# Hybrid decoder step: Delta heads and retention or mLSTM heads in turn

## What is computed

```
x += rms(W_out [mLSTM | retention | gated Delta](rms(x)))
x += rms(W_down relu(W_up rms(x))^2)

# a Delta head, per chunk
q3,k3,v3 = split(silu(conv4(q,k,v)));  q = l2norm(q3)*d**-.5;  k = l2norm(k3)
A   = strict(decay) * beta * k k^T
sol = (I + A)^-1 [beta*gamma*k, beta*v];  U = Ut - W S
o   = gamma * q S + (q k^T * decay) U
S   = exp(G) S + (k * decay)^T U
```

## Time and profile before

| | us |
|---|---|
| median of 3 runs (lowest, highest) | 3278.93 (3278.43, 3280.37) |
| the profiled execution | 3280.49 |
| its span, first to last instruction | 3278.9 |
| mean granted TensorE clock | 0.987 of full speed |
| head quads, one layer | about 40 to 675 |
| weight loads (256 KB each) | 1669, 3.7 from issue to landing |

### The profile page before, as it was taken

One profiled execution on the slowest core, in us unless ns is written; L12 is line 12 of the kernel. 1 busy time (PEld: TensorE's weight loads), 2 busy tenths in 40 slices (PEclk: granted clock), 3 DMA queues, 4 the chain that ended last, 5 costly groups with the idle time before them and its releaser, 6 DMA issues.

```text
span 3278.9 us, 72394 instructions
## 1 busy us (share of the span) xinstructions
PE 3122.5 (95%) x23264; PEld 3057.9 (93%) x23264; DVE 1930.1 (59%) x3923; ACT 1535.4 (47%) x3564; POOL 84.5 (3%) x161
## 2 busy tenths in 40 slices
PE   5999999998999999999869999999989999999997
PEld 5989999998999999999869989999989999999997
DVE  5677755656545545455567777556665455454555
ACT  4566654544433334334446666545444333343333
POOL 0000000000000000000010000000000000000000
PEclk9999999999999999999989999999999999999999
DMA  3344455643544444544423444555435444444454
GB/s 132 128 133 135 132 162 161 185 155 110 175 166 159 164 164 166 166 160 164 151 84 121 131 132 137 168 167 177 155 118 167 165 164 167 162 163 164 163 167 147
DMA packets 266061, 499.24 MB, mean 152 GB/s; under 512 B 34272, under 2 KB 39552, under 8 KB 265664
## 3 DMA queue, kind: packets, MB, share of 16 engines
q1 hardware_dynamic: 243360, 443.56, 41.3%
q0 software_dynamic: 14496, 51.05, 4.7%
q10 hardware_dynamic: 8064, 2.80, 0.3%
HBM read 475.30 MB, written 22.01 MB: 152 GB/s over the span
## 4 chain that ended last, share of the span: by engine, by line
PE 79%; DVE 9%; ACT 5%; issue 4%; DMA 2%; DVEq 1%; ACTq 0%; SPq 0%; POOLq 0%; POOL 0%
PE PU L455 71%; PE PABCD L455 4%; PE PE_ L455 2%; ACT Y L787 2%; PE PF L455 2%; ACT AE L787 1%; DVE WL L1156 1%; DMA RAW<-in_w 1%; ACT WH L787 1%; DVE Y L1170 1%; PE PABCD L458 1%; DVE Y L1321 1%; DVE AE L1500 1%; DVE X L1173 0%; PE PE_ L458 0%
## 5 line engine op out<-in xcount | busy, mean ns | idle before, releaser
L455 PE MATMUL PU<-HH,WH 128*128 128x288 f32 x4096 | 1285.4, 314 | 59.3 <-DVE HL L1161 48.0
L787 ACT ACTIVATE WH<-RAW 128x512 fp32r<-128x512 f32 x1669 | 965.2, 621 | 591.9 <-PE PU L455 437.5
L455 PE MATMUL PU<-HL,WH 128*128 128x288 f32 x4096 | 1212.6, 296 | 0.0
L455 PE MATMUL PU<-HH,WL 128*128 128x288 f32 x4096 | 1208.7, 295 | 0.0
L1156 DVE TENSOR_TENSOR WL<-RAW,WH 128x512 fp32r<-128x512 f32 x1668 | 1074.5, 687 | 223.0 <-ACT WH L787 205.8
L455 PEld LDWEIGHTS PU<-HH,WH 128*128 128x128 f32 x4096 | 774.6, 189 | 79.2 <-DVE HL L1161 49.4
L455 PEld LDWEIGHTS PU<-HL,WH 128*128 128x128 f32 x4096 | 775.8, 189 | 7.0
L455 PEld LDWEIGHTS PU<-HH,WL 128*128 128x128 f32 x4096 | 775.0, 189 | 0.0
L455 PE MATMUL PU<-UH,WH 128*128 128x288 f32 x2560 | 759.0, 296 | 3.2 <-DVE UL L1310 2.0
L455 PE MATMUL PU<-UL,WH 128*128 128x288 f32 x2560 | 755.2, 295 | 0.0
L455 PE MATMUL PU<-UH,WL 128*128 128x288 f32 x2560 | 752.7, 294 | 0.0
(11 more groups left out here) (245 smaller groups left out, 2244.4 us busy)
## 6 DMA issues: line engine op xcount, KB each, us to landing
RAW<-in_w SPq DMA_DIRECT2D x1669, 256.0 KB, 3.7
SIN<-in_sin POOLq DMA_DIRECT2D x32, 512.0 KB, 4.2
out_sout<-Y POOLq DMA_DIRECT2D x32, 512.0 KB, 5.3
BC<-gate_rows POOLq DMA_DIRECT2D x32, 304.0 KB, 4.3
AUX<-in_aux POOLq DMA_DIRECT2D x32, 152.0 KB, 3.4
X<-in_x SPq DMA_DIRECT2D x4, 576.0 KB, 7.5
out_y<-X SPq DMA_DIRECT2D x4, 576.0 KB, 2.8
Y<-in_gw POOLq DMA_DIRECT2D x2, 1024.0 KB, 5.0
```

What stands on the lines that cost most here:

```text
L455: return nc.tensor.matmul(out, lhsT, rhs, start=start, stop=stop, skip_group_check=True)
L787: return nc.scalar.activation(out, in_, f, **kw)
```

## The change

`walk` now pairs the heads: a Delta head's quad, then a retention head's (first four pairs) or an mLSTM head's (next three), with the front of the next Delta head in it. The last pair is Delta head 7's quad, without a front, and mLSTM head 3 in the first "out" quad. `par` is 0 for every Delta head and 1 for every other. Weights, states and parameters stay in memory where they were, so SP and POOL take their addresses from the new order; TensorE waits for the output blocks by `turn_of`. The silu semaphore is split in two.

```diff
-                def gdn_pair(i, last):
-                    for par in range(2):
-                        h = 2 * i + par
-                        after = None if last and par else (n0 + h + 1, l * H_C + h + 1, h + 1, 1 - par, p0 + i + par)
-                        quad(q0 + 1 + h, "gdn", l, (n0 + h, l * H_C + h, h, par, p0 + i), after)
...
-                with eng.Fori(0, H_B // 2) as i:
-                    for par in range(2):
-                        h = 2 * i + par
-                        quad(q0 + 1 + H_C + h, "ret", l, (n0 + H_C + h, l * H_B + h, h, par, p0 + H_C // 2 + i))
-                for h in range(H_A - 1):
-                    quad(q0 + 1 + H_C + H_B + h, "mls", l, (n0 + H_C + H_B + h, l * H_A + h, h, h % 2, p0 + (H_C + H_B + h) // 2))
...
+                def pair(i, other, k):
+
+                    g0 = l * H_C
+                    quad(q0 + 1 + 2 * i, "gdn", l, (n0 + 2 * i, g0 + i, i, 0, p0 + i))
+                    quad(q0 + 2 + 2 * i, other, l, (n0 + 2 * i + 1, l * H_B + k, k, 1, p0 + i),
+                         (n0 + 2 * i + 2, g0 + i + 1, i + 1, 0, p0 + i + 1))
+
+                with eng.Fori(0, H_B) as i:
+                    pair(i, "ret", i)
+                for i in range(H_B, H_C - 1):
+                    pair(i, "mls", i - H_B)
+                i = H_C - 1
+                quad(q0 + 1 + 2 * i, "gdn", l, (n0 + 2 * i, l * H_C + i, i, 0, p0 + i))
+                last_head = (n0 + 2 * i + 1, l * H_A + H_A - 1, H_A - 1, 1, p0 + i)
...
+        def turn_of(k):
+
+            return 2 * k if k < H_C else 2 * (k - H_C) + 1
...
+            with sp.Fori(0, DEPTH) as l:
+                q0, u0 = l * QUADS, l * (4 * QUADS)
+
+                with sp.Fori(0, H_C - 1) as i:
+                    next_units(q0 + 2 * i, u0 + 4 * i, u0 + 4 * (H_C + i))
+                    next_units(q0 + 2 * i + 1, u0 + 4 * (H_C + i), u0 + 4 * (i + 1))
...
-                if next_head:
+                if next_at is not None:
 
                     held("head_done", n + 1)
-                    load_parameters(n + 1, 1 - par)
-                    load_rows(n + 1, 1 - par)
...
+                    load_parameters(next_at, 1 - par)
+                    load_rows(next_at, 1 - par)
...
-                            pe.wait_ge(sem("ul_ready"), ul_before(l, kind, x[0]) + k + 1)
+                            pe.wait_ge(sem("ul_ready"), ul_before(l, kind, x[0]) + (turn_of(k) if kind == "out" else k) + 1)
...
-                    tt(HHD[:], YY, Z[par][:, 3], ALU.mult).then_inc(sem("y_gated"), 1)
+                    tt(HHD[:], YY, Z[par][:, 3], ALU.mult).then_inc(sem(f"{silu}_y_gated"), 1)
```

More of the change, by code:

```diff
@@ L344, in _, with next_units @@
                 sp.dma_start(con[n][:], d[n]).then_inc(sem("constants_in"), 16)
-            with sp.Fori(0, DEPTH * QUADS) as Q:
+            def next_units(Q, unit, after):
                 for s in range(4):
@@ L349, in _ @@
                         sp.wait_ge(sem("lo_ready"), 16 * Q + 4 * s + c + 1)
-                        load(c, 4 * Q + s + 1)
+                        load(c, unit + s + 1 if s < 3 else after)
+            with sp.Fori(0, DEPTH) as l:
[3 more added lines that the diff above has]
+                    next_units(q0 + 2 * i + 1, u0 + 4 * (H_C + i), u0 + 4 * (i + 1))
+                i = H_C - 1
+                next_units(q0 + 2 * i, u0 + 4 * i, u0 + 4 * (H_C + i))
+                next_units(q0 + 2 * i + 1, u0 + 4 * (H_C + i), u0 + 4 * HEADS)
+                with sp.Fori(HEADS, QUADS) as q:
+                    next_units(q0 + q, u0 + 4 * q, u0 + 4 * (q + 1))
             sp.wait_ge(sem("lo_ready"), 16 * DEPTH * QUADS + 1)
@@ L382, in load_state, with head @@
                 pool.dma_start(SIN[:].rearrange("p b e -> p (b e)"), one("sin", n)).then_inc(sem("state_in"), 16)
-            def head(l, n, pair, par, next_head):
-                if next_head:
+            def head(n, at, next_at, pair, par):
+                if next_at is not None:
                     held("head_done", n + 1)
-                    load_parameters(n + 1, 1 - par)
-                    load_rows(n + 1, 1 - par)
-                if next_head:
+                    load_parameters(next_at, 1 - par)
+                    load_rows(next_at, 1 - par)
+                if next_at is not None:
                     held("state_decayed", n + 1)
                     held("state_read", n + 1)
-                    load_state(n + 1)
+                    load_state(next_at)
                 held("state_ready", n + 2)
-                pool.dma_start(one("sout", n)[:, HD:], CDEC.rearrange("p b e -> p (b e)")).then_inc(sem("state_out"), 16)
+                pool.dma_start(one("sout", at)[:, HD:], CDEC.rearrange("p b e -> p (b e)")).then_inc(sem("state_out"), 16)
                 held("state_out", 16 * (n + 1))
@@ L441, in _ @@
                 pool.dma_start(NG0[:], one("ng0", l + 1)).then_inc(sem("first_gain_in"), 16)
-                with pool.Fori(0, (H_C + H_B) // 2) as i:
-                    for par in range(2):
-                        head(l, n0 + 2 * i + par, p0 + i, par, True)
-                for h in range(H_A):
-                    head(l, a0 + h, p0 + (H_C + H_B) // 2 + h // 2, h % 2, h < H_A - 1)
+                with pool.Fori(0, H_C - 1) as i:
+                    head(n0 + 2 * i, n0 + i, n0 + H_C + i, p0 + i, 0)
+                    head(n0 + 2 * i + 1, n0 + H_C + i, n0 + i + 1, p0 + i, 1)
+                i = H_C - 1
+                head(n0 + 2 * i, n0 + i, n0 + H_C + i, p0 + i, 0)
+                head(n0 + 2 * i + 1, n0 + H_C + i, None, p0 + i, 1)
             pool.wait_ge(sem("first_gain_in"), 16 * (DEPTH + 1))
@@ L920, in head_scale, with linear_head @@
                 fn(GATE[:], LG[:], ACT.Exp, scale=-1.0).then_inc(sem("head_scale"), 1)
-            def linear_head(step, kind, x, last):
+            def linear_head(step, kind, l, x, last):
                 n, nk, hk, par, pair = x
@@ L1077, in gdn_head @@
                 if t == 27:
-                    store_prompt_state(n)
+                    store_prompt_state(n, l * HEADS + hk)
                     act.wait_ge(sem("gdn_out"), nk + 1)
@@ L1086, in mixer @@
                 if kind == "gdn":
-                    gdn_head(t, x)
+                    gdn_head(t, l, x)
                 elif kind in ("ret", "mls"):
@@ L1093, in mixer @@
                         if t == slot:
-                            linear_head(step, kind, x, last)
+                            linear_head(step, kind, l, x, last)
                 elif kind == "first":
@@ L1405, in linear_head @@
                     finish_log(n)
-                    y = finish_rest(n, par, not mls)
+                    y = finish_rest(n, par, None if mls else kind)
                     if not mls:
-                        dve.wait_ge(sem("y_gated"), silu_count(l, kind, hk))
+                        dve.wait_ge(sem("ret_y_gated"), nk + 1)
                     store_u(n, l, chunk_of(kind, hk), y)
@@ L1478, in gdn_tail @@
                 n, nk, hk, par, pair = x
-                y = finish_rest(n, par, True)
-                dve.wait_ge(sem("y_gated"), silu_count(l, "gdn", hk))
+                y = finish_rest(n, par, "gdn")
+                dve.wait_ge(sem("gdn_y_gated"), nk + 1)
                 store_u(n, l, chunk_of("gdn", hk), y)
```

15 lines of the change are left out of this document (4 added, 11 removed).

## The result

The changed kernel took **3285.70 us** (median of 14 runs, 3283.35 to 3288.21), the kernel before 3279.37 (14 runs): a ratio of **1.0017, 95% interval 1.0010 to 1.0025**, so 6.3 us slower. The forecast was 3269.5 and faster. The range, 3252 to 3294, holds the result; the direction was wrong. A second comparison, on another chip, gave 1.0014 (1.0005 to 1.0023).

The account below looks back on a forecast made before the run. TensorE was taken as the bound, busy for 95% of the span, with removable waits. -47.0 + 14.4 + 19.2 + 3.9 = -9.5 us from 3280.49 gave 3271.0, less 1.56 for the median: 3269.5 us; range 3252 to 3294.

Parts of the forecast that it names:

- The pool: TensorE's waits at four lines, 39.2 us listed in 49 waits, 47.0 us with 0.16 added each, all taken off.
- Retention quads: Eight retention quads with a front: new TensorE waits of 0.1 and 1.7 us, 1.8 us each, 14.4 us in all.
- excluded `WL`: Unit matmuls would not wait for WL; if they did, the weights' own chain had slipped and the forecast was wrong.
- The Delta quad near 41 us: Sign of being right: a Delta quad, 44.60 us long before the change, would take near 41 us.
- near 36: Sign of being right: a retention quad, 33.97 us long before the change, would take near 36 us.
- the root is then no longer late: Delta quad behind a fronted retention quad: root ready at 482.4, wanted at 480.9 + 1.7, so no further wait.
- mLSTM quads: Six mLSTM quads with a front: waits of 0.45, 1.5 and 1.2 us, 3.2 us each, 19.2 us in all.
- Out quad: First slot of two out quads: TensorE waits 1.9 us for Delta head 7's tail, 3.9 us in all.
- A: Rival: VectorE sets the fronted quads, 4 us each, +13 us, 3292 us; decides from 3.1 us per quad; chance 0.23.
- B: Rival: no change; full durations instead of spacings make CUR and UL about 0.7 us later, +10, 3279 us; chance 0.27.
- C: Rival: much faster; fronts find gaps in short quads, new waits half the size, -26, 3253 us; chance 0.16.
- The rule weighed: Skill: improve the busiest engine (no gain here), or interleave regimes (gain); trace bears out the latter for 1.4% of span.

Follow-up runs that it names:

- control run: The changed kernel unaltered, run once more beside the second group of experiments: 3288.11 us, 1.0014 of the kernel before.
- e4_cur_early: Changed kernel with CUR written in slot 22 instead of 31 of the 14 fronted retention and mLSTM quads: 3287.63 us, ratio 1.0003 to the kernel before.
- e2_v_one_tap: Changed kernel with three of the four v-channel taps left out in every front: 3272.66 us, ratio 0.9956 to the kernel before.
- e5_cnew_early: Changed kernel with the copies to CNEW and their store moved from slots 30 and 31 to 25 and 26: 3282.64 us, ratio 0.9999 to the kernel before.
- e1_last_wait: Changed kernel with TensorE's out-quad wait for Delta head 7 moved from slot 0 to slot 3: 3284.13 us, ratio 0.9991 to the kernel before.
- e6_store_late: Changed kernel with the retention or mLSTM head's store moved from slot 24 to 30, behind the v taps: 3265.79 us, ratio 0.9952 to the kernel before.
- e7_three: Changed kernel with head store in slot 30, CNEW copies in slots 25 and 26, out-quad wait in slot 3: 3265.54 us, ratio 0.9948 to the kernel before.
- e13_unrolled: Changed kernel with late head store, CUR in slot 22, out-quad wait in slot 3; then VectorE's retention-pair loop written out: 3250.42 us, ratio 0.9898.

## Why the prediction was wrong

**The pool, 47.0 us.** Right in kind: the waits of the earlier trace rows that I took off are gone, but for the root, which I priced anew. One root wait of the pool (0.63 + 0.16 us) stands behind the "first" quad of the second layer, which the change leaves as it was (0.36 in the control run), so up to 0.8 us too much was taken off.

**Retention quads, 14.4 us; measured 8 x 2.84 = 22.7.** Up to the k-k product my chain is close, and the retention quad ends on TensorE at 162.1 where it was to end at 162.0. On the scale of the earlier trace rows (head 0's sum 312.09 us later there) `UL` was to end at 160.1 and ended at 160.2; `KS4` was to come at 166.1 and came at 166.2; TensorE was to lose 1.7 us by then and lost 1.14 at `WL` and 0.57 at k-k, 1.71. I had the sum right and the first of the two places wrong: I had excluded `WL`, and said that such waits would show the weights' chain slipped. It did slip, but took only what k-k would have taken. The Delta quad near 41 us that I named as a sign is 43.4 long, since all three waits fall into it, and the retention quad is 34.1 and not near 36.

**The step that failed is "the root is then no longer late".** I let the decay start at `CUR` (167.1 forecast, 167.8 measured) and left out what ScalarE has in its own list behind `KS4`: two weight tiles, the copies to CNEW, their store and a copy of v, until 168.62. By this the root was ready at 171.85 and not at 170.3, and TensorE paid 0.97 + 0.16 = 1.13 us again. The same omission stands in the mLSTM step ("1.0 late by itself and so hidden in that"). Together 8 x 1.13 + 6 x 1.11 = 15.7 us. `e4_cur_early` shows that `CUR` isn't the limit, `e2_v_one_tap` that the wait doesn't come from the lateness ahead of k-k, and `e5_cnew_early` that a shorter list of ScalarE takes 8.5 us of the root waits away. Of the 5.1 us left there, the part behind retention heads (3.1 us) is set by VectorE's own list between the evacuation and `AM`, which the step left out as well.

**mLSTM quads, 19.2 us; measured 6 x 4.08 = 24.5.** Without the root 2.97 us, against my 3.2: 0.71 at the head sum (forecast 0.45), 1.16 at the second norm sum (1.5), 1.10 at `WL` and k-k (1.2).

**Out quad, 3.9 us; measured 4.6 in the waits,** 3.0 by the span of `e1_last_wait`. Right.

**The sum.** -47.0 + 0.8 + 22.7 + 24.5 + 4.6 = +5.6 us, beside +6.0 measured by the spans. The forecast plus the missing 15.7 would have been +6.2, and it is this term that turned "faster" into "slower"; the others were off by 1.4 us or less each.

**The rivals.** A came true in its direction (+13 forecast, +6.3 measured by the medians), at 3.4 us for each fronted quad against its threshold of 3.1. Its reason, that VectorE is too full (87 and 93% of a quad), was not the point: `e6_store_late` leaves all that work in and is 22 us faster. It was the order of VectorE's list, and ScalarE's. B's reason (full durations in place of spacings) is not borne out: `UL` and `KS4` came within 0.1 us, and the subtraction's follower still starts 0.61 us behind it (160.44 to 161.05). `CUR` did come 0.7 late, but nothing waited for it. C was half true: the fronts' steps do find their gaps, once the store stands behind them.

**The rule weighed.** I had drawn on the Trainium skill (Perfetto Trace Analysis, Identifying the Most-Contended Engine and Optimization Strategy): interleaving regimes with different busy engines may help. In these runs the loads became more even (windows above) and the time rose by 0.17%; the gain of 0.8 to 1.0% came only with the order inside the quads and the written-out loop. The trace agrees with the rule only under that condition.

## What to carry to other kernels

Before two in-order programs are laid beside each other, list for every engine what stands ahead of the steps that another engine will wait for next, also the copies and stores that nobody waits for, and put work whose result is needed late (here a head's store) behind work that is needed soon. A wait that another wait covers today returns in full if the two sides between them have fixed lengths; price each place by the later of all the lists that feed it. An edit is worth what the latest list allows: writing `CUR` early left the root wait as it was when done alone, and gave 8 to 9 us once VectorE's list was the later one, and moving the copy to CNEW gave 5.5 us alone, nothing beside the others, and cost 15 us in quads whose slot was full.

## What was not expected of the hardware

Starting a store on ScalarE's queue is not free for ScalarE: behind the last copy to CNEW it was idle for 0.67 us, of which the 0.34 of the DMA's issue are a part, and the next weight tile stood behind it. In `e7_three`, with copy and store moved away, the two weight tiles follow each other without idle time. And the end of a loop has a price on the engine that runs it: VectorE stood for 0.91 us behind the evacuation that closes the loop's body and for 0.35 with the same body written out (`e13_unrolled`), 0.56 us each time round. It reached the time because VectorE's list set the next wait; for three rounds in two layers it is 3.4 of the 6.1 us that writing the loop out gave.
